# The second mixer: copies shared anew, the residual loaded late, the odd chunks' states copied by ScalarE for all groups in four pieces

## What is computed

```python
def s5_mixer(h, hc, ...):
    u, u_c = grp(h), grp(hc)                # 64 groups of 16 channels; hc is the context
    y = u * d
    for di, rev in enumerate((False, True)):
        lam_bar = jnp.exp(lam * jnp.exp(log_step[di]))
        h0 = zeros                           # 64 complex states a group
        yc_d, h_ctx = s5_scan(u_c, lam_bar, b_bar, c_mat, h0, rev, need_ctx)
        yl_d, _ = s5_scan(u, lam_bar, b_bar, c_mat, h_ctx, rev, True)
        y = y + yl_d
    z = gelu(y)
    val, gt = split(z @ glu_w + glu_b)
    return val * sigmoid(gt)
# around it
h = modulate(rms_norm(x, norm1_g[1]), sh1, sc1)     # hc from ctx in the same way
x = x + g1 * y
```

## Time and profile before

| | us |
|---|---|
| median of 3 runs | 2512.29 (2508.50 to 2512.55) |
| the profiled execution | 2506.16 |
| its span | 2504.4 |
| TensorE (PE) busy | 2143.6 (86%) |
| VectorE (DVE) busy | 1092.3 (44%) |
| ScalarE (ACT) busy | 509.8 (20%) |
| GpSimd (POOL) busy | 433.9 (17%) |

### The profile page before, as it was taken

How to read it: one execution, slowest core, us unless ns; L and a number is a source line. 1 busy time by engine, 2 the same in 40 slices (tenths; PEclk the granted TensorE clock), 3 DMA queues, 4 the chain that set the end, 5 groups by cost and what they waited for, 6 DMA issues and landing times. The chain is left out here.

```text
span 2504.4 us, 40476 instructions
## 1 busy us (share of the span) xinstructions
PE 2143.6 (86%) x11989; PEld 1189.9 (48%) x11990; DVE 1092.3 (44%) x2311; ACT 509.8 (20%) x945; POOL 433.9 (17%) x359
## 2 busy tenths in 40 slices
PE   5889999997999999999999816699789999988874
PEld 3765444744544444444444405354444444444442
DVE  8853365944543333333333338942532222222222
ACT  3443233611121111111111125220221111100000
POOL 1000000002012222222222210000122222232332
PEclk9999999998999999999999968799799999999997
DMA  9971002003799999999999669830499999899996
GB/s 358 386 265 46 34 34 84 1 1 131 264 346 355 354 358 357 359 351 350 355 358 358 202 158 329 275 146 0 160 404 375 361 363 358 274 390 372 385 385 207
DMA packets 173622, 666.72 MB, mean 266 GB/s; under 512 B 37666, under 2 KB 48898, under 8 KB 129882
## 3 DMA queue, kind: packets, MB, share of 16 engines
q1 hardware_dynamic: 121410, 564.71, 58.7%
q0 software_dynamic: 36160, 64.84, 11.0%
q10 hardware_dynamic: 15960, 35.96, 4.1%
HBM read 617.29 MB, written 86.09 MB: 281 GB/s over the span
## 5 line engine op out<-in xcount | busy, mean ns | idle before, releaser
L1518 PE MATMUL banks_l<-slotw_l,xTw_l 128*128 128x512 f32 x800 | 358.2, 601 | 27.7 <-issue 27.7
L1529 PE MATMUL banks_l<-slotn_l,xTn_l 128*64 128x256 f32 x2816 | 325.0, 383 | 34.5 <-issue 34.5
L1529 PEld LDWEIGHTS banks_l<-slotn_l,xTn_l 128*64 128x64 f32 x2816 | 212.0, 137 | 178.9 <-issue 104.8
L1518 PEld LDWEIGHTS banks_l<-slotw_l,xTw_l 128*128 128x128 f32 x800 | 148.5, 191 | 239.3 <-issue 239.3
L1568 PE MATMUL banks_l<-slotn_l,late_l 128*64 128x512 f32 x704 | 189.9, 615 | 19.6 <-DVE late_l L1356 17.9
L1547 PE MATMUL banks_l<-slotw_l,late_l 128*128 128x512 f32 x400 | 191.8, 602 | 15.4 <-DVE late_l L1338 15.4
L977 POOL DMA_INDIRECT xgw_l<-moe_h,idxw_l x58 | 60.6, 1045 | 741.0 <-PE banks_l L1463 367.1
L1005 POOL DMA_INDIRECT moe_acc<-late_l,idxn_l x88 | 151.2, 1718 | 190.5 <-DMA moe_acc<-late_l,idxn_l 172.5
L937 POOL IOTA slotw_l<- 128x1 f32 x2 | 0.3, 140 | 729.1 <-POOLq L69 431.3
L1335 DVE TENSOR_TENSOR late_l<-late_l,banks_l 128x256 f32<-128x256 f32 x50 | 21.0, 421 | 240.2 <-ACT late_l L1107 240.2
L556 PE MATMUL ps_a<-W_a,hT_a 128*128 128x512 f32 x288 | 124.9, 595 | 0.0
(11 more groups left out here) (433 smaller groups left out, 3235.0 us busy)
## 6 DMA issues: line engine op xcount, KB each, us to landing
slotn_l<-in_exp_w_gate SPq DMA_DIRECT2D x88, 1024.0 KB
slotn_l<-in_exp_w_up SPq DMA_DIRECT2D x88, 1024.0 KB
slotn_l<-in_exp_w_down SPq DMA_DIRECT2D x88, 1024.0 KB, 12.1
slotw_l<-in_exp_w_gate SPq DMA_DIRECT2D x50, 1024.0 KB
slotw_l<-in_exp_w_up SPq DMA_DIRECT2D x50, 1024.0 KB
slotw_l<-in_exp_w_down SPq DMA_DIRECT2D x50, 1024.0 KB
w_p<-in_mod_w SPq DMA_DIRECT2D x12, 2048.0 KB, 15.4
W_a<-in_ar_w_in SPq DMA_DIRECT2D x5, 2048.0 KB, 9.4
```

Source lines behind the costliest of these rows:

```text
L1518: last = pe.matmul(pGU_w, xT_w[b % 2][:, k, :], wgu[0][b % WIDE_RING][:, :, k, :], start=(k == 0), stop=(k == KD - 1))
L1529: last = pe.matmul(pGU_n[H * side:H * side + H, b % 2], xT_n[b % 2][:, k % 4, H * (k // 4):H * (k // 4) + H], w[:, :, k, P * side:P * side ...
```

## The change

- **Loads.** ScalarE issues the vector DMAs ahead of the second copy. SyncE no longer waits for the sums before the fifth R block. The residual is not taken from X any more: both copies are loaded anew from DRAM, the first into x before the second GLU half, the second into XR (in XS) after the last from_states, and DVE adds them in the first GLU unit.
- **Weight tiles.** The slots w are in another order (XS first), tile 0 is issued before U is written, tiles 1 and 2 after it.
- **Evictions.** ScalarE does the ctx copy for 11 of the 16 half batches, DVE for half batches 2, 5, 8, 11 and 14. A sweep is no longer cut into thirds: DVE does per batch its ctx copies, then all four operations.
- **States.** The states that come from odd chunks are copied for all groups by ScalarE in four pieces (16, 8, 4 and 4 steps, each for both directions), which wait for the step that they need and stand behind the four row copies in ScalarE's program. Per batch only every second chunk is left: ScalarE the forward ones, and the backward ones of batches 1, 3, 5 and 7, DVE the others. The scratch of the steps moves from XS to the end of Rall.
- SyncE loads W tiles 3 and 4 after modulation 6 instead of 8, and DVE has 57 small memsets before the GLU instead of 50.

```diff
@@ -2065,7 +2065,8 @@
         g1 = UV[:, KD * 2 * D:KD * 2 * D + D]
-        w = [v.rearrange("p (k n) -> p k n", k=HK) for v in (ZU[:, 0], ZU[:, 1], XS[:, SG * NCL:])]
+        w = [v.rearrange("p (k n) -> p k n", k=HK) for v in (XS[:, SG * NCL:], ZU[:, 0], ZU[:, 1])]
+        XR = XS[:, 0:NL * D].rearrange("p (m d) -> p m d", m=NL)
         flat = x[:].rearrange("p t d -> p (t d)")
@@ -2086,6 +2087,25 @@
         XN_DVE, R_ACT = 5, 2
+        PIECES = ((0, 16), (16, 24), (24, 28), (28, 32))
+        ACT_BACK = (1, 3, 5, 7)
+        def by_act(b):
+            return b + 1 + sum(k <= b for k in ACT_BACK)
+        def by_dve(b):
+            return b + 1 - sum(k <= b for k in ACT_BACK)
+        DVE_CTX = (2, 5, 8, 11, 14)
+        def evicted(hb):
+            return 3 * (hb + 1) - ctx_copied(hb)
+        def ctx_copied(hb):
+            return sum(k <= hb for k in DVE_CTX)
+        def tile_rows(part, m, hh):
+            return part.rearrange("(m h c) d -> m h c d", m=NL, h=2)[m, hh, 0:NCL, :]
         CTX_OPS, STEPS = 4 * 4, NCL // 2 - 1
@@ -2112,11 +2132,6 @@
             for hb in range(R_ACT, NHB):
-                if hb == 4:
-                    sp.wait_ge(S['x_sum'], SL)
-                    for m in range(NL):
-                        for hh in range(2):
-                            sp.dma_start(x[hh * 64:hh * 64 + 64, m, :], X[0:64, 2 * m + hh, :]).then_inc(S['xres_in'], 16)
                 if hb >= NR:
@@ -2139,7 +2154,7 @@
             toeplitz(LATE - 1)
-            sp.wait_ge(S['mod_mm'], LATE)
+            sp.wait_ge(S['mod_mm'], LATE - 2)
             for b in range(3, NW):
@@ -2155,13 +2170,20 @@
                 sp.dma_start(Wb[b % NW], io['s5_w'][:, b]).then_inc(w_in[b % NW], 16)
-            sp.wait_ge(S['sf_done'], NB)
-            sp.wait_ge(S['sb_done'], NB)
+            sp.wait_ge(S['sf_done'], by_act(NB - 1))
+            sp.wait_ge(S['sb_done'], by_dve(NB - 1))
             for b in range(2):
...
             sp.dma_start(g1, io['modrow'][1, 0:1, 2 * D:3 * D].to_broadcast([P, D])).then_inc(S['gb_in'], 16)
+            for m in range(NL):
+                for hh in range(2):
+                    sp.dma_start(x[hh * 64:hh * 64 + 64, m, :], tile_rows(parts[0], m, hh)).then_inc(S['xres_in'], 16)
             glu_half(1)
+            sp.wait_ge(S['o_mm'], NB)
+            for m in range(NL):
+                for hh in range(2):
+                    sp.dma_start(XR[hh * 64:hh * 64 + 64, m, :], tile_rows(parts[1], m, hh)).then_inc(S['xres_in'], 16)
@@ -2176,12 +2198,12 @@
         def _(act):
+            for s in range(2):
+                act.dma_start(vec[:, 2 * s:2 * s + 2], io['modrow'][1, s, 0:2 * D].rearrange("(a g j) -> g a j", a=2, j=SI)).then_inc(S['vec_in'], 16)
+            act.dma_start(vec[:, 4], io['norm1_g'][1].rearrange("(g j) -> g j", j=SI)).then_inc(S['vec_in'], 16)
             for j in range(2):
...
                    .then_inc(x_in[j], 16)
-            for s in range(2):
-                act.dma_start(vec[:, 2 * s:2 * s + 2], io['modrow'][1, s, 0:2 * D].rearrange("(a g j) -> g a j", a=2, j=SI)).then_inc(S['vec_in'], 16)
-            act.dma_start(vec[:, 4], io['norm1_g'][1].rearrange("(g j) -> g j", j=SI)).then_inc(S['vec_in'], 16)
             act.dma_start(lam[:, 0].rearrange("p a b g -> p (a b g)"), io['s5_l8']).then_inc(S['l8_in'], 16)
@@ -2204,6 +2226,9 @@
                    .then_inc(S['xn_act'], 1)
+            act.wait_ge(S['xn_done'], XN_DVE)
+            act.wait_ge(S['xn_act'], SL - XN_DVE)
+            act.dma_start(w[0], mod_weights(io, *MOD_LATE[0], 0)).then_inc(m_in[0], 16)
             act.wait_ge(S['vec_done'], 1)
@@ -2213,20 +2238,25 @@
                 last.then_inc(S['u_act'], 1)
-            act.wait_ge(S['xres_in'], 16 * 8)
-            for n in range(3):
+            for n in range(1, 3):
                 act.dma_start(w[n], mod_weights(io, *MOD_LATE[n // 2], n % 2)).then_inc(m_in[n], 16)
...
                 act.activation(VH[0:64, 0:NCC, :, gs].rearrange("p c a g -> p g a c"), v_of(hb)[0:64, :, :, NCK:P], ACT.Copy).then_inc(S['va_done'], 1)
+                if hb not in DVE_CTX:
+                    act.activation(VH[64:P, 0:NCC, :, gs].rearrange("p c a g -> p g a c"), v_of(hb)[64:P, :, :, 0:NCC], ACT.Copy)\
+                       .then_inc(S['va_done'], 1)
...
                 act.wait_ge(S['fill'], 4 * (b + 1))
-                act.activation(SV[0:64, :, g, :], VH[0:64, NCC - 1:NCK - 1, :, g].rearrange("p c a g -> p a g c"),
+                act.activation(SV[0:64, :, g, 1::2], VH[0:64, NCC:NCK - 1:2, :, g].rearrange("p c a g -> p a g c"),
                                ACT.Copy).then_inc(S['sf_done'], 1)
+                if b in ACT_BACK:
+                    act.activation(SV[64:P, :, g, 0::2], VH[64:P, NCK - 2:NCC - 1:-2, :, g].rearrange("p c a g -> p a g c"),
+                                   ACT.Copy).then_inc(S['sf_done'], 1)
@@ -2247,6 +2277,13 @@
                        .then_inc(row_out[u % 2], 16)
+            for k0, k1 in PIECES:
+                act.wait_ge(S['rec'], CTX_OPS + 4 * max(k1 - 1, 0) + 1)
+                act.activation(SV[0:64, :, :, 2 * k0:2 * k1:2], VH[0:64, NCC - 1 + 2 * k0:NCC - 1 + 2 * k1:2].rearrange("p k a g -> p a g k"),
+                               ACT.Copy).then_inc(S['even_copied'], 1)
+                act.activation(SV[64:P, :, :, NCL - 2 * k1 + 1:NCL - 2 * k0:2],
+                               VH[64:P, NCC - 3 + 2 * k1:NCC - 2 + 2 * k0 if k0 else NCC - 2:-2].rearrange("p k a g -> p a g k"),
+                               ACT.Copy).then_inc(S['even_copied'], 1)
             for b in range(3):
@@ -2332,8 +2369,9 @@
                         dve.wait_ge(S['up'], n)
-                    dve.wait_ge(S['va_done'], 4 * (b + 1))
-                    dve.wait_ge(S['vd_done'], 2 * (b + 1))
+                    dve.wait_ge(S['va_done'], evicted(2 * b + 1))
+                    if ctx_copied(2 * b + 1):
+                        dve.wait_ge(S['vd_done'], ctx_copied(2 * b + 1))
                     dve.tensor_tensor(a, even, factor(0, 0, NPAIR, g), ALU.mult).then_inc(S['up'], 1)
@@ -2344,17 +2382,13 @@
-            dve.wait_ge(S['xres_in'], 16 * 8)
-            for hb in range(NHB):
-                dve.wait_ge(S['va_done'], 2 * hb + 1)
-                dve.tensor_copy(VH[64:P, 0:NCC, :, 4 * hb:4 * hb + 4].rearrange("p c a g -> p g a c"), v_of(hb)[64:P, :, :, 0:NCC])\
-                   .then_inc(S['vd_done'], 1)
-                if 2 <= hb < 14:
-                    b, third = divmod(hb - 2, 3)
-                    sweep(b, third)
-                    if third == 2:
-                        sweep(b, 3)
-            for b in range(4, NB):
+            dve.wait_ge(S['xn_act'], SL - XN_DVE)
+            for b in range(NB):
+                for hb in (2 * b, 2 * b + 1):
+                    if hb in DVE_CTX:
+                        dve.wait_ge(S['va_done'], evicted(hb - 1) + 1)
+                        dve.tensor_copy(VH[64:P, 0:NCC, :, 4 * hb:4 * hb + 4].rearrange("p c a g -> p g a c"), v_of(hb)[64:P, :, :, 0:NCC])\
+                           .then_inc(S['vd_done'], 1)
                 for stage in range(4):
@@ -2380,7 +2414,7 @@
                 prev, here = VH[:, NCC - 1 + 2 * q], VH[:, NCC + 1 + 2 * q]
-                a, b = t1[:, q % 2], t2[:, q % 2]
+                a, b = (Rall[:, WN + (2 * (q % 2) + j) * 2 * SG:WN + (2 * (q % 2) + j + 1) * 2 * SG].rearrange("p (a g) -> p a g", a=2) for j in range(2))
                 dve.wait_ge(S['rec'], at)
@@ -2406,7 +2440,7 @@
                 g = slice(b * GB, (b + 1) * GB)
-                dve.tensor_copy(SV[64:P, :, g, :], VH[64:P, NCK - 2:NCC - 2:-1, :, g].rearrange("p c a g -> p a g c"))\
+                dve.tensor_copy(SV[64:P, :, g, 0::2], VH[64:P, NCK - 2:NCC - 1:-2, :, g].rearrange("p c a g -> p a g c"))\
                    .then_inc(S['sb_done'], 1)
@@ -2417,15 +2451,15 @@
                 dve.wait_ge(S['fill'], 4 * (b + 1))
-                states(b)
+                if b not in ACT_BACK:
+                    states(b)
             dve.wait_ge(S['o_mm'], NW)
...
                 turned(b)
-            for _ in range(50):
+            for _ in range(57):
                 done(dve.memset(sqr[:, 0, 0, 0:1], 0.0))
...
             dve.wait_ge(S['gb_in'], 32)
-            dve.wait_ge(S['xres_in'], 16 * 8)
             for u in range(8):
@@ -2441,6 +2475,11 @@
                 done.wait()
+                if u == 0:
+                    dve.wait_ge(S['xres_in'], 16 * 16)
+                    for t in range(NL):
+                        done(dve.tensor_tensor(x[:, t, :], x[:, t, :], XR[:, t, :], ALU.add))
+                    done.wait()
                 done(dve.tensor_tensor(x[:, m, c], x[:, m, c], a, ALU.add))
@@ -2470,8 +2509,9 @@
                 if hb >= 4:
-                    pe.wait_ge(S['va_done'], 2 * (hb - 3))
-                    pe.wait_ge(S['vd_done'], hb - 3)
+                    pe.wait_ge(S['va_done'], evicted(hb - 4))
```

(15 more changed lines are left out.)

## The result

The changed kernel takes 2519.88 us in the median (2517.15 to 2527.10, 10 runs), the kernel before 2506.07 us beside it (2501.97 to 2512.63, 10 runs). The ratio is 1.0052, with a 95% interval of 1.0039 to 1.0065: 13 us slower. Forecast was 9.6 us slower, 2521.9 us from the median of 2512.3 shown then. The profiled execution took 2522.34 us, its span is 2520.6 us.

What follows compares the result with a forecast made beforehand. Two chains of nearly equal length, DVE's work and TensorE's modulations, were taken to bound the mixer stage. +2.0, +3.4, +16.0 + 1.1, less 7.7 and 5.2, gave +9.6 us: 2521.9 from 2512.3, range 2505 to 2528.

Steps and rivals of the forecast that it cites:

- Start: Start of the mixer: R blocks 4 to 6 beside the second copy delay DVE's last sum by 2.0 us; vector DMAs cost nothing.
- Evictions and sweeps: DVE drops 11 of 16 ctx copies, 7.1 us; at 0.97 us a sweep operation its steps end 3.8 us earlier.
- The fifth copy and the cold clock: DVE's fifth ctx copy behind sweep 6 delays TensorE's first Toeplitz product, with a slow clock after it: +3.4 us.
- rival 1: The modulation chain hardly moves, paced by bytes, and R blocks cost nothing: +4 us, 2516; chance 0.33.
- Pieces: ScalarE's eight copies of odd-chunk states, behind modulation 8 and ahead of from_states(0): 16.0 us, bounds 8.4 and 24.
- rivals 2: Faster: pieces cost the plain 0.85 ns, 8.4 us, and the modulation chain ends 1 to 3 us earlier: -6, 2506; chance 0.17.
- 3 (24 us): Slower still: strided writes on top of strided reads make the pieces 24 us: +17.6, 2530; chance 0.08.
- Waits behind the pieces: Between from_states(0) and the GLU, TensorE's waits for the gelus behind ScalarE and DVE go: -5.2 us.
- Residual: In the GLU, 16 residual loads and four DVE additions, 4.8 us together, fit beside the first products: nothing.

Runs made afterwards that it cites:

- The double copy: The changed kernel with all eight copies of the pieces done twice, same data to the same place: 2532.83 us, ratio 1.0113 to the kernel before.
- the last two versions: Changed kernel, SyncE's wait and vector DMAs back, pieces 1, 2 halved early, GLU half behind W tiles; the second also fifth ctx copy earlier: 2506.10 and 2506.21 us.

## Why the prediction was right

The forecast's sign, its mechanism and its largest term held; two smaller terms were off in opposite directions. That the sum came within 3.4 us of the measured 13.0 is in part luck: the start cost 3.7 us more than forecast, the fifth copy 2.0 us less.

- **Start.** Forecast +2.0, bounds 0 and 4.9; measured +5.7 for the last sum, beyond the upper bound. This is the step that failed. I priced the R blocks alone, at what they could take from the last 4.9 us of the second copy, and the vector DMAs at nothing. Alone they measured +2.3 and +0.7. Together, in the changed kernel, they measured +3.5 to +7.0. Why the two combine to more than their sum is open: the one run that puts the vector DMAs back and keeps the early R blocks shows an earlier last sum, 35.4, close to the 35.8 of R blocks alone, and the same time.
- The Trainium skill ("DMA: Bandwidth & Descriptors", section "Queues, rings and completion order") has each DMA engine serve the queues in turn, by which I had worked out 4.9 us. R blocks alone cost 2.3 us, half of that; the changed kernel's 5.7 lies above it. Neither run isolates the rule.
- **Evictions and sweeps.** DVE was to be through with its steps at 141.3, and was at 143.8, late by what the start was late beyond the forecast (3.7 us) less 1.2. The 1.2 us are a price that was too high: a sweep operation took 0.92 us here (1541.52 to 1545.18 for four), not 0.97. In part that was a miscount, since the 38.9 us before hold 13 copies, not 12, which gives 0.95. The levels and steps kept their length: 42.93 us from the last sweep's end, against 42.89. The gain of fewer ctx copies is real, 7 us, and DVE spent it waiting: the first fill stood 5.72 us idle for modulation 8.
- **The fifth copy and the cold clock.** By the chain's end forecast +3.4, measured +1.4 (7.04 less the start's 5.68). Four parts make the difference of 2.0. The first Toeplitz product: 4.9 of its own forecast (6.9 less 2.0), 3.9 measured, by the same price of a sweep operation. Product, bias and modulation: 5.8 forecast, 4.8 measured (1561.93 to 1566.74), since the clock had recovered by the first modulation. From the issue of tile 3 to the product on Toeplitz tile 2: 11.5 forecast, 12.2 measured (1566.74 to 1578.97); before it took 15.3, with the DMA engines full of other loads (share 1.10). From there to the end of the chain: 35.9 forecast, 35.1 measured. So rival 1 was right that part of the delay is given back on the way, but not that the chain hardly moves. What the fifth copy's place is worth stays open: with the copy moved forward the profiles show nothing once and 2 us once, and the times settle neither.
- **Pieces.** Forecast 16.0 us, starting 2.8 us behind the last modulation. Measured 16.3 us (1616.96 to 1633.24), starting 2.9 us after it ended (1614.11), with DVE's last step 8.4 us past. 64x2048 takes 3.82 us, 3.8 was forecast. From the last row copy to from_states(0) it took +10.0, forecast +9.4. The double copy shows that the pieces end the path, and piece 1 ahead of the fourth row copy that their place in ScalarE's program puts them there. The measured length rules out the prices of rivals 2 (8.4 us) and 3 (24 us). The forecast rightly subtracted the 7.7 us that stood there before.
- The Trainium skill ("Advanced Engine Details and Errata", section "SBUF Cachelines") wants two hits on a 16-byte line for full speed. The measured 3.82 us for 2048 elements, less the 0.17 fixed of the prediction, is 1.78 ns an element, the same as with contiguous writes: writes 8 bytes apart added nothing, as that rule has it.
- **Waits behind the pieces.** Forecast -5.2 between from_states(0) and the GLU; measured -4.5 (26.84 against 31.38). The first product took 6.28 us instead of 5.04.
- **Residual.** It cost nothing, as forecast: the additions waited 11.73 us for their loads, and the GLU's products span 109.5 us before and after.

The sum: +5.7 start, +1.4 copy and clock, +10.0 pieces, -4.5 waits: +12.6, against +2.0, +3.4, +9.4 and -5.2: +9.6. The two profiled executions differ by 16.2 us, of which 3.4 us are the later start of the mixer; the ratio of 1.0052 is 13.0 us, so I take those 3.4 us for chance. The terms come from one profile of each kernel. The start alone took from +3.5 to +7.0 with the same loads, so that 12.6 meets 13.0 this closely is chance as well.

One reading of the page was off: its digits drop in slices 24 to 26, and slice 27 has a 9 again. Nothing was worked out from it.

Open: the GLU 3 to 5 us earlier in single profiles of the last two versions shows in no median. Executions of one kernel lie up to 17 us apart, and the tail from the last GLU product to the end takes 745 to 752 us from profile to profile, so a few microseconds in one profile of each can't be told from that. The kernel before with the vector DMAs first is an example: in its profile the GLU is 4 us late, 2.64 us of it a wait for a W tile, and its median shows no loss.

## What to carry to other kernels

A copy lies under another engine's work only if its own engine's program order lets it start there. The wait on the step had passed for 8 us before the pieces ran, because a row copy that belongs to another chain stood ahead of them. (The weight tile in XS would have held them until modulation 7 in any case; only the real halves are free of it.) Time taken from one of two chains of equal length is spent waiting for the other: DVE's 7 us became 5.7 us of idle. What ends a path can be paid in full and still not be worth its length: behind the pieces stood the last Toeplitz tile, and by the idle in this profile only 9 of their 16 us could be had back. And an earlier consumer can find the next transfer late. Here TensorE waited for loads on SyncE's queue in most repairs (1.96 us, 0.36, 5.03, then 2.22), and the order on the queue was to blame for the longest, since changing it ended that wait. Not every such wait comes from a repair, as the 2.64 us above show.

## What the runs showed of the hardware beyond that

- Three small vector DMAs ahead of the second copy (3 MB in four pairs) on ScalarE's queue delayed the first sum by 9 us (18.1 instead of 9.2) and the last by 0.7. The cause of the 9 us was not looked for.
- from_states behind a wait for its tile took 3.58 us (wait of 1.96) and 3.68 us (5.03) instead of 1.97, at a granted clock of 0.50: 1.6 and 1.7 us on top of the wait. It isn't so each time. In the changed kernel a Toeplitz product behind a wait of 3.06 us took 1.09 us, at a clock of 1.00.
- The same 32 matmuls of the first modulation took 2.03 us in the changed kernel, where the clock was back at 1.00 at 1565 us, and 3.42 in the one with the fifth copy earlier, where it stood at 0.50 until 1564 us. The gap before was 6.44 us in the first and 3.89 in the second, so the longer gap did not cost more here.
